# The last shift projection tile spread over the recurrence's first slots, and half of the recurrence's turns as TensorE transposes

## What is computed

```python
u_hy, u_rw, g_hy, g_rw = jnp.split(h @ w_in, split_at, axis=-1)
...
def _centred_token_shift(u, mu):
    return u + mu[0] * (prev - u) + mu[1] * (nxt - u)

def _rwkv7_step(S, inp):
    r, w, k, v, kk, a = inp
    sa = jnp.einsum('dbhij,dbhj->dbhi', S, -kk)
    S = S * w[..., None, :] + sa[..., None] * (kk * a)[..., None, :] + v[..., None] * k[..., None, :]
    y = jnp.einsum('dbhij,dbhj->dbhi', S, r)
    return S, y
```

## Time and profile before

| | us |
|---|---|
| median of three runs | 2919.23 (2918.84 to 2919.31) |
| the profiled execution, its own time | 2922.75 |
| its span, first to last instruction | 2921.0 |
| TensorE busy in the span | 2863.0 (98%) |
| VectorE busy | 1467.3 (50%) |
| ScalarE busy | 1085.4 (37%) |
| mean granted TensorE clock | 0.997 |

### The profile page before, as it was taken

How to read it: one execution, slowest core, us unless ns; L and a number is a source line. 1 busy time by engine, 2 the same in 40 slices (tenths; PEclk the granted TensorE clock), 3 DMA queues, 4 the chain that set the end, 5 groups by cost and what they waited for, 6 DMA issues and landing times.

```text
span 2921.0 us, 43018 instructions
## 1 busy us (share of the span) xinstructions
PE 2863.0 (98%) x19334; PEld 2365.6 (81%) x19334; DVE 1467.3 (50%) x1431; ACT 1085.4 (37%) x1176; POOL 174.8 (6%) x94
## 2 busy tenths in 40 slices
PE   9999999999999999999999999999998998999998
PEld 7787788888889888888888888788877886888886
DVE  6766553443454544343454344555666555544432
ACT  5554532222454732222342223442244432332222
POOL 1002110000100010000110000330000000100001
PEclk9999999999999999999999999999999999999999
DMA  4220022323222022223222233321240003222222
GB/s 148 73 76 2 30 87 101 101 90 119 101 90 87 30 87 88 100 101 108 101 98 90 101 103 112 112 80 65 87 133 4 3 5 133 87 101 101 98 98 79
DMA packets 44887, 249.06 MB, mean 85 GB/s; under 512 B 8443, under 2 KB 12283, under 8 KB 17184
## 3 DMA queue, kind: packets, MB, share of 16 engines
q1 hardware_dynamic: 43552, 242.11, 24.2%
q10 hardware_dynamic: 1152, 4.19, 0.4%
HBM read 237.90 MB, written 8.39 MB: 84 GB/s over the span
## 4 chain that ended last, share of the span: by engine, by line
PE 91%; DVE 5%; ACT 3%; issue 1%; DMA 0%; POOL 0%; SPq 0%; DVEq 0%; ACTq 0%
PE ps L667 75%; PE ps L2909 6%; PE ps L1522 1%; PE ps L2493 1%; PE ps L2203 1%; PE ps L3961 1%; PE ps L2477 1%; PE ps L3944 1%; PE ps L3973 1%; PE ps L2174 0%; PE ps L3083 0%; DVE wlo L274 0%; DVE gdn_conv L1147 0%; ACT whi L268 0%; PE ps L426 0%
## 5 line engine op out<-in xcount | busy, mean ns | idle before, releaser
L274 DVE TENSOR_TENSOR wlo<-wraw,whi 128x2048 fp32r<-128x2048 f32 x210 | 486.5, 2317 | 911.0 <-ACT whi L268 906.9
L268 ACT ACTIVATE whi<-wraw 128x2048 fp32r<-128x2048 f32 x210 | 402.1, 1915 | 900.1 <-PE ps L667 900.1
L667 PE MATMUL ps<-ffn_xh,whi 128*128 128x512 f32 x1408 | 549.2, 390 | 0.2 <-DVE wlo L274 0.2
L667 PE MATMUL ps<-ffn_xh,wlo 128*128 128x512 f32 x1408 | 547.8, 389 | 0.0
L667 PE MATMUL ps<-ffn_xl,whi 128*128 128x512 f32 x1408 | 547.8, 389 | 0.0
L667 PEld LDWEIGHTS ps<-ffn_xh,whi 128*128 128x128 f32 x1408 | 264.3, 188 | 57.0 <-DVE wlo L274 1.0
L667 PEld LDWEIGHTS ps<-ffn_xl,whi 128*128 128x128 f32 x1408 | 264.3, 188 | 55.6 <-issue 0.7
L667 PEld LDWEIGHTS ps<-ffn_xh,wlo 128*128 128x128 f32 x1408 | 264.3, 188 | 54.7
L667 PE MATMUL ps<-ffn_uh,whi 128*128 128x512 f32 x704 | 274.1, 389 | 0.0
L667 PE MATMUL ps<-ffn_uh,wlo 128*128 128x512 f32 x704 | 273.9, 389 | 0.0
L667 PE MATMUL ps<-ffn_ul,whi 128*128 128x512 f32 x704 | 273.9, 389 | 0.0
(11 more groups left out here) (518 smaller groups left out, 4485.9 us busy)
## 6 DMA issues: line engine op xcount, KB each, us to landing
wraw<-in_weights SPq DMA_DIRECT2D x211, 1024.0 KB, 4.9
gates_kept<-gates_tmp ACTq DMA_DIRECT2D x8, 512.0 KB, 4.1
mix_gate<-gates_kept SPq DMA_DIRECT2D x8, 512.0 KB, 11.2
h<-in_x SPq DMA_DIRECT2D x4, 512.0 KB, 8.3
mix_y<-hz_kept SPq DMA_DIRECT2D x2, 1024.0 KB, 6.4
out<-out SPq DMA_DIRECT2D x4, 512.0 KB, 3.1
wraw<-in_weights SPq DMA_DIRECT2D x2, 512.0 KB, 6.7
ple_raw<-in_p SPq DMA_DIRECT2D x4, 256.0 KB, 5.2
```

The costliest lines, as they stand in the source:

```text
L268: c.nc.scalar.activation(c.whi[:, j % 2, :], c.wraw[:, j % 2, :], ACT.Copy).then_inc(c.hi_ready, 1)
L274: c.nc.vector.tensor_tensor(c.wlo[:, j % 2, :], c.wraw[:, j % 2, :], c.whi[:, j % 2, :].bitcast(F32), ALU.subtract).then_inc(c.lo_ready, 1)
L667: last = nc.tensor.matmul(pair[:, m, :], a, b, start=opens and n == 0 and wa + xa == 0, stop=closes and n == len(ks) - 1 and wa == 1)
```

## The change

The tile that was last in the projection is left out of `shift`'s own loops on TensorE, ScalarE and VectorE (`deferred=1`). Its 16 units are issued from the recurrence: two before slot 0, then after the build of slots 0 to 8 of stage 0, up to unit 4, 6, 8, 10, 11, 13, 14, 15 and 16. Its evacuation stands at slot 9 on VectorE and on ScalarE. As `hy_x` is then still being read, pair 0 has buffers of its own for `LT`, `X`, `Y` and `MQ`, and one `vt` buffer lies elsewhere. The wait on `free` of the last tile but one moves to `pe_keys`. Pair 0's preparation is moved on: ScalarE's steps 16 on from after tile 6 to after tile 5, VectorE's steps 17 to 19 likewise. The first step of ScalarE's preparation of a later pair waits for `kd` instead of `A`.

The second part: in the three places that turn by the identity, the product of the first head (partitions 0 to 63) becomes a transpose instruction of TensorE; that of the second head stays a matmul.

```diff
@@ Dense.scalar, Dense.vector, Dense.tensor
-        for r in range(len(self.body)):
+        for r in range(len(self.body) - self.deferred):
...
@@ Recurrence.__init__
-        self.vt = [put(f"vt{b}", [P, NCH, C7], at) for b, at in enumerate((69632, 111424))]
+        self.vt = [put(f"vt{b}", [P, NCH, C7], at) for b, at in enumerate((69632, 6144))]
...
+        early = 16384 + 8192 * (shift.last_parity == 0)
+        self.LT = [c.ring("rw_LT0", small, early)] + [put("LT", small, 123712)] * (HP - 1)
+        self.X = [c.ring("rw_X0", small, early + 4096)] + [put("X", small, 127808)] * (HP - 1)
+        self.Y = [put("Y0", small, 2048)] + [put("Y", small, 136000)] * (HP - 1)
+        self.MQ = [put("MQ0", [P, NCH, 2 * C7], 2048)] + [put("MQ", [P, NCH, 2 * C7], 136000)] * (HP - 1)
...
@@ Recurrence.tensor
         self.misc_read = self.at("vtc", 0)
+        last = len(RW_ORDER) - 1
+        self.shift.tensor_ahead(pe, last, 2)
         pe.wait_ge(*self.misc_read)
-        last = len(RW_ORDER) - 1
-        pe.wait_ge(*self.shift.free(last - 1))
...
+                if k == 0 and s < 9:
+                    self.shift.tensor_ahead(pe, last, (4, 6, 8, 10, 11, 13, 14, 15, 16)[s])
...
+    def turned(self, out, src):
+
+        nc, ident, (one, two) = self.c.nc, self.c.ident, self.halves()
+        nc.tensor.transpose(out(one), src(one), ident[one, one])
+        return nc.tensor.matmul(out(two), src(two), ident[two, two], start=True, stop=True)
...
@@ pe_keys
             pe.wait_ge(*self.at("Bt", k - 1))
+        else:
+            pe.wait_ge(*self.shift.free(len(RW_ORDER) - 2))
...
@@ pe_turn
-                last = self.both(lambda r: self.bank(banks[d])[r, n, :], lambda r: src[r, d, n, :],
-                                 lambda r: self.c.ident[r, r])
+                last = self.turned(lambda r: self.bank(banks[d])[r, n, :], lambda r: src[r, d, n, :])
...
@@ scalar_beside
-        for s in {2: range(1), 3: range(1, 7), 4: range(7, 13), 5: range(13, 16), 6: range(16, SLOTS)}.get(r, ()):
+        for s in {2: range(1), 3: range(1, 7), 4: range(7, 13), 5: range(13, SLOTS)}.get(r, ()):
...
@@ scalar
+                if k == 0 and s == 9:
+                    self.shift.act_evac(act, len(RW_ORDER) - 1, len(RW_ORDER) - 1)
...
@@ act_prepare
             if p:
-                act.wait_ge(*self.at("A", 2 * p - 1))
+                act.wait_ge(*self.at("kd", p - 1))
...
@@ vector_beside
-        for s in {3: range(8), 4: range(8, 12), 5: range(12, 17), 6: range(17, SLOTS)}.get(r, ()):
+        for s in {3: range(8), 4: range(8, 12), 5: range(12, 20), 6: range(20, SLOTS)}.get(r, ()):
...
@@ vector
+                if k == 0 and s == 9:
+                    self.shift.dve_evac(dve, len(RW_ORDER) - 1, len(RW_ORDER) - 1)
...
@@ second_half
-                 order=RW_ORDER, late=2)
+                 order=RW_ORDER, late=2, deferred=1)
```

More of the change, by code:

```diff
@@ L1063, in __init__ @@
     def __init__(self, c, name, n, norm, dst, padded, taps, pad, bias=None, func=None, conv=None, beside=(),
-                 beside_pe=(), held=0, first=True, dst_free=None, order=None, late=0):
-        self.late = late
+                 beside_pe=(), held=0, first=True, dst_free=None, order=None, late=0, deferred=0):
+        self.late, self.deferred = late, deferred
         self.beside, self.beside_pe, self.held, self.dst_free = beside, beside_pe, held, dst_free
@@ L3008, in pe_values @@
             for n in range(NCH):
-                last = self.both(lambda r: out[r, n, :], lambda r: self.MQ[r, n, i * C7:(i + 1) * C7],
+                last = self.both(lambda r: out[r, n, :], lambda r: self.MQ[k][r, n, i * C7:(i + 1) * C7],
                                  lambda r: vt[r, n, :])
@@ L3027, in pe_left @@
         for n in range(NCH):
-            last = self.both(lambda r: out[r, n, :], lambda r: self.LT[r, d, n, :], lambda r: self.X[r, d, n, :])
+            last = self.both(lambda r: out[r, n, :], lambda r: self.LT[k][r, d, n, :], lambda r: self.X[k][r, d, n, :])
         last.then_inc(*self.done("Y"))
@@ L3088, in pe_prepare @@
             for n in range(NCH):
-                last = self.both(lambda r: out[r, n, :], lambda r: u[r, 2 * HP + p, n * C7:(n + 1) * C7],
-                                 lambda r: self.c.ident[r, r])
+                last = self.turned(lambda r: out[r, n, :], lambda r: u[r, 2 * HP + p, n * C7:(n + 1) * C7])
             last.then_inc(*self.done("vt"))
@@ L3102, in pe_finish @@
             for n in range(NCH):
-                last = self.both(lambda r: out[r, n, :], lambda r: self.yp[r, n, :], lambda r: self.c.ident[r, r])
+                last = self.turned(lambda r: out[r, n, :], lambda r: self.yp[r, n, :])
             last.then_inc(*self.done("turn"))
@@ L3183, in act_left @@
             act.wait_ge(*self.at("Z", 10 * k + 2 * (l - 1) + d))
-        self.c.nc.scalar.activation(self.Y[:, d, :, :], self.bank(self.y_bank(d)), ACT.Copy).then_inc(*self.done("Yc"))
+        self.c.nc.scalar.activation(self.Y[k][:, d, :, :], self.bank(self.y_bank(d)), ACT.Copy).then_inc(*self.done("Yc"))
     def act_prepare(self, act, p, s):
@@ L3336, in dve_build @@
             dve.wait_ge(*self.at("XTi", 2 * k + d))
-            nc.vector.transpose(self.X[:, d, :, :], XT).then_inc(*self.done("Xi"))
+            nc.vector.transpose(self.X[k][:, d, :, :], XT).then_inc(*self.done("Xi"))
         if s in (2, 5):
```

17 lines of the change are left out of this document (9 added, 8 removed).

## The result

The changed kernel takes 3031.42 us (median of 4 runs, 3030.42 to 3036.5) against 2919.27 us of the kernel before in the same session: a ratio of 1.0384, with a 95% interval of 1.0366 to 1.0402. Some 112 us came on top. I had forecast 2920.4, with a range of 2915.8 to 2925.0. The forecast was wrong, by far, and on the side to which I had given one chance in ten.

What follows compares the result with a forecast made beforehand. TensorE's own work was taken as the bound. The tile's terms, -1.49 + 1.5 + 0.2 + 1.0 = +1.2 us, plus 0 for the turns, put 2919.2 at 2920.4 us, range 2915.8 to 2925.0.

Steps and rivals of the forecast that it cites:

- What bounds the kernel: Whole kernel: only shortening TensorE's own work or filling its waits can move the time; TensorE busy 2863.0 of 2921.0 us.
- The turns: 192 pairs turned by the identity: the transposed half hides behind the full matmul; 0 us, upper end +0.9.
- Rival 2: Turns: alternating transpose and matmul costs like a change of form, 0.18 us a pair, 35 us, 2955; chance 0.04.
- Rival 3: Granted clock: stage 1's drop to half goes (2916.0, chance 0.06) or a second comes (2924.8, chance 0.08).
- rival 4: Turns: transposes leave TensorE half idle, so the clock falls in each stage; 4 x 4.4 us, 2938; chance 0.03.
- The other page: Turns: if the column-tiling rule made the float32 transpose an ordinary matmul, the turn and the sum would stay the same.
- The tile: Deferred tile's units spread over slots 0 to 8 of stage 0: -1.49 + 1.5 + 0.2 + 1.0 = +1.2 us.
- The waits in slots 1 to 8: Stage 0 on TensorE: the units fill three waits of 1.02, 0.21 and 0.26 us; gain 1.49 us.
- 0.2 for `vtc`: Start of the recurrence: without the tile ahead, TensorE's first group waits for `vtc`; loss 0.2 us.
- ten changes of form: Slots 0 to 9: added switches between 64x64 groups and wider units, 0.15 us each, 1.5 us lost; bounds 0.5 to 3.0.
- The evacuation: Slot 9, VectorE: standing between level 0's two `rw_X`, it delays the second; loss 1.0 us, none at best.
- rivals 1: Turns: a pair costs by its records, three instead of four, so 5.7 us go, 2914.7; chance 0.09.

Runs made afterwards that it cites:

- e6: Kernel before with no transposes: in each turn all products of the first head, then all of the second; 2937.4 us, ratio 1.0062.
- e4: Kernel before with all 192 pairs changed, but in each turn all transposes of the first head first, then all products of the second; 2934.8 us, ratio 1.0058.
- e5: Kernel before with all 192 pairs changed, in groups of four transposes, then four products, 48 groups in all; 2961.0 us, ratio 1.0144.
- e7: Kernel before without transposes: the second head's product issued as two of 32 columns, so the tile's form changes twice a pair; 3048.3 us, ratio 1.0443.
- e3: Kernel before with only the turns of the values and of the output changed, 64 pairs instead of 192; 2962.2 us, ratio 1.0149.
- e2: Kernel before with only the turns changed, in all 192 pairs, and nothing of the tile; 3028.7 us, ratio 1.0375.
- e10: Kernel before with each product of the turns issued four times over in the old order, no transposes or changes of form; 2986.2 us, ratio 1.0229.
- e1: Changed kernel with the turns put back to two products, so the tile's move alone; 2924.2 us, ratio 1.0013.
- e9: The tile's move alone, turns by two products, with the tile's evacuation in slot 15 instead of 9 on both engines; 2920.1 us, ratio 1.0003.

## Why the prediction was wrong

**What bounds the kernel.** Right. TensorE's own work sets the time, and all 112 us lie in TensorE's busy time.

**The turns.** This is the step that failed, at the sentence "The pair is bound by each quadrant's own passes, and the shorter half hides behind the longer. I take 0". The term was 0 with bounds of -5.7 and +0.9. The first half of the sentence holds: in e6 one quadrant's records follow each other after 0.059 us, so that two of them take the 0.118 of a pair. The second half does not. The term is 0.31 us a pair: two switches of 0.13 (e4, e5), and about 0.05 because three records in a row on different quadrants no longer run side by side (3 x 0.058 instead of 0.118; e6 shows that this goes with the order). Hiding needs the two halves to be under way together, and in the change the product starts 0.17 us after the transpose beside it (2174.47 to 2174.64). The upper bound looked only at a slower pace of records; the price of a switch, which I had worked out myself as 0.09 to 0.15 us for the tile, belonged in it. 192 x 2 x 0.15 = 58 us would have been the honest upper end.

**Rival 2** was the right mechanism, and e7 shows it in its general form. It was mis-sized (0.18 a pair, measured 0.31), and it got 0.04 on the strength of one row: four whole-array transposes with products right behind them and "no extra time". That row is read rightly: on the whole array the step from a transpose to a product costs nothing there. But it cannot exclude a price on quadrants, and that the two differ so is a finding of these runs; why they do stays open. It stood beside rows of 64x64 groups next to wide ones, which did show a price; those were nearer to the case. Where one row shows a price and another none, the range has to reach the price.

**The clock.** Nearly half of the loss, some 50 us, and in no term of mine. Rival 3 knew that a wait can let the clock fall, rival 4 that turns might; neither was joined to rival 2. Rival 2's 35 us were pairs alone, yet pairs with such gaps bring falls of the clock with them: in e3 20 us of pairs bring 23 of clock, in e5 some 23 (48 groups of 0.945 - 4 x 0.118 each) bring 19, in e2 60 bring 49. e10 has pairs as long and no gaps, and loses nothing but their length. Rival 4 had the turns as the place, but its cause is not needed, and its 4.4 us for each stage were far too few. The Trainium skill (TensorE: Matmul & The Clock Gate, Part 4: PE-mode transpose) has it that transposes don't count as a busy engine in the same way; with none of them in the turns the mean falls to 0.81 (e7), and with all 192 in runs of 8 or 16 it stays at 0.99 (e4). So the gaps are enough, and they are nearly all of it. That transposes add a little is not excluded: e4 has falls behind its turns and e6 none, and e4's median lies 2.5 us above its two executions without a fall.

**The other page** (the Trainium skill, TensorEngine Tiling (Array Packing), Gotcha 2: Feature Incompatibilities) I had read as: if the rule made the transpose an ordinary matmul, nothing would change. The trace decides against that reading. In e2 a turn has 48 records instead of 64, and a transpose takes one pass. The Trainium skill's rule that column tiling and the transpose mode for float32 exclude each other was a warning against this change all the same, if not one with a price.

**The tile.** Forecast +1.2 us, measured +1.63 up to the turn of `B` (e1). The waits in slots 1 to 8 went, 1.49 us, as said. The start of `pe_strict` was right to 0.01, so 0.2 for `vtc` holds. That leaves 0.77 + 1.49 - 0.2 = 2.1 us for ten changes of form, 0.21 each instead of the 0.15 taken, inside the bounds of 0.05 and 0.3. Read directly, the first island of e1 has 0.33 for its two changes, close to the 0.30 forecast; the rest comes by subtraction and was not traced to its places. The evacuation cost 0.9 (e9) instead of 1.0. A term of this size was missing from the whole: with the evacuation in slot 9 the clock is lower in nearly every execution (in the profiled one it falls first at the place where it fell in the profile of before), and this is most of the 5 us of e1. In the window of slot 12 TensorE now waits 2.08 us; that the longer wait is what brings the fall in stage 1, some 57 us later, has not been shown.

**The range** left out rivals 1, 2 and 4 with 0.16 together. A larger chance for them would not have been enough: the highest price on the list was rival 2's 2955, and the kernel takes 3031. What was missing was rival 2 at its full size together with the clock.

## What to carry to other kernels

On the quadrants of TensorE, count switches before records: each step between a transpose and a product, or between tiles of different form, cost 0.12 to 0.2 us here, as much as two to four records of 64x64. A cheaper instruction put between dearer ones of another kind is no saving; if both kinds are needed, put them in runs, and look at what the run costs in overlap of the quadrants (products alone: 0.118 a pair alternating, 0.21 in runs). In no run here did transposes on quadrants beat the two products in alternation. And where a change lengthens a stretch by gaps inside TensorE's busy time, add the clock to its price: here that nearly doubled it, while the same length full of work cost only its length.

## What the runs showed of the hardware

- Two 64x64 float32 products on opposite quadrants take 0.118 us together if issued in alternation, and 0.21 if all of one quadrant come first (e6).
- A float32 transpose of 64x64 on a quadrant takes 0.058 us in a run of its kind, about half of a product's two passes; the switch to a product and back takes 0.24 to 0.26 us (e4, e5, the change).
- A switch to 32 columns costs about as much as one to a transpose: 0.49 us for a pair that needs 0.118 without (e7).
- The granted clock went to 0.50 behind eight pairs of a transpose and a product (2174.47 to 2177.89 in the change), though projection matmuls at full clock stood ahead of them, and it was at 0.50 for 56 us where waits and turns followed. Each us at 0.50 cost about 0.35 us of the kernel's time (the change, e2, e3, e5, e7).
- The page shows TensorE as 98% busy with the change as before it, though a turned pair has three records in 0.43 us where it had four in 0.118: "busy" counts the time in which a record is open.
- On the whole array, four transposes and the products behind them show no price of a switch; on quadrants there is one.
